# Two pairs of outputs of the last projection's second input half as seven block products, with residual rows at the end and moves around the pooled rows

## The reference, cut to what matters

```python
for l in range(DEPTH_2):
    u = rms_norm_2(h, norm_in_g[l])
    proj = jnp.einsum('bsd,de->bse', u, w_in[l])
    pool_x, pool_z, m_x, m_z = jnp.split(proj, ...)
    y_pool = pool_mixer(pool_x, pool_w[l], pool_scale[l]) * jax.nn.silu(pool_z)
    y_m = mlstm_branch(m_x, ...) * jax.nn.silu(m_z)
    y = jnp.concatenate([y_pool, y_m], axis=-1)
    h = h + jnp.einsum('bse,ed->bsd', y, w_out[l])
return rms_norm_2(h, norm_out_g)
```

## Time and profile before

| | before |
|---|---|
| time, median of 3 runs | 1710.2 us (1709.71 to 1710.64) |
| profiled execution | 1709.35 us, of which the profiler's span is 1707.6 |
| PE busy | 1664.8 us, 97% of the span, 8119 matmuls |
| DVE busy | 1277.2 us, 75% |
| ACT, POOL busy | 726.9 us (43%), 540.7 us (32%) |
| granted clock of PE, mean | 0.996 of full speed |

### The profile page before, as it was taken

One profiled execution on the slowest core, in us unless ns is written; L12 is line 12 of the kernel. 1 busy time (PEld: TensorE's weight loads), 2 busy tenths in 40 slices (PEclk: granted clock), 3 DMA queues, 4 the chain that ended last, 5 costly groups with the idle time before them and its releaser, 6 DMA issues.

```text
span 1707.6 us, 21819 instructions
## 1 busy us (share of the span) xinstructions
PE 1664.8 (97%) x8119; PEld 1375.5 (81%) x8119; DVE 1277.2 (75%) x1556; ACT 726.9 (43%) x933; POOL 540.7 (32%) x409
## 2 busy tenths in 40 slices
PE   8999999999999999999999999999999999999997
PEld 6888888887788888887788877788788788878885
DVE  7987888435677777777775799878888367789764
ACT  7211113225556655566622423511124667683203
POOL 5344544332201011111022323335344322217541
PEclk9999999999999999999999999999999999999998
DMA  6012125141010111101432354112226611344432
GB/s 231 25 75 75 46 91 209 62 169 42 25 38 1 37 38 38 36 3 38 166 113 99 113 183 149 64 68 81 75 88 202 244 50 63 124 162 159 173 111 99
DMA packets 51321, 164.93 MB, mean 97 GB/s; under 512 B 6272, under 2 KB 6912, under 8 KB 50960
## 3 DMA queue, kind: packets, MB, share of 16 engines
q1 hardware_dynamic: 50928, 163.01, 26.8%
q10 hardware_dynamic: 288, 0.52, 0.1%
HBM read 122.49 MB, written 41.03 MB: 96 GB/s over the span
## 4 chain that ended last, share of the span: by engine, by line
PE 81%; DVE 13%; ACT 3%; issue 2%; DMA 0%; POOL 0%; SPq 0%; DVEq 0%; POOLq 0%; ACTq 0%
PE pair L1212 27%; PE pair L1737 10%; PE pair L1399 9%; PE pair L1473 9%; PE pair L1536 5%; PE aux L1509 4%; PE pair L1522 3%; PE pair L1903 1%; PE aux L1688 1%; DVE stat_b L2995 1%; PE pair L1223 1%; PE pair L1888 1%; PE pair L1231 1%; PE aux L1649 1%; PE aux L1859 1%
## 5 line engine op out<-in xcount | busy, mean ns | idle before, releaser
L1046 POOL CAST w_hi<-w_raw 128x1024 fp32r<-128x1024 f32 x66 | 81.0, 1228 | 751.5 <-issue 561.7
L1048 POOL TENSOR_TENSOR w_lo<-w_raw,w_hi 128x1024 fp32r<-128x1024 f32 x66 | 173.1, 2622 | 5.3
L1212 PE MATMUL pair<-op_hi,w_hi 128*128 128x512 f32 x446 | 138.7, 392 | 1.0 <-ACTq L185 1.0
L1212 PE MATMUL pair<-op_lo,w_hi 128*128 128x512 f32 x446 | 137.9, 391 | 0.0
L1212 PE MATMUL pair<-op_hi,w_lo 128*128 128x512 f32 x446 | 137.7, 390 | 0.0
L2210 ACT ACTIVATE pt_hi<-pair 128x1024 fp32r<-128x1024 f32 x60 | 61.6, 1027 | 126.6 <-issue 84.3
L2627 DVE TENSOR_TENSOR pt_lo<-pair,pt_hi 128x1024 fp32r<-128x1024 f32 x60 | 73.5, 1225 | 52.0 <-ACT pt_hi L2210 48.5
L1473 PE MATMUL pair<-opb_hi,w_hi 128*128 128x512 f32 x256 | 101.9, 398 | 1.1 <-DVEq L185 0.6
L1212 PEld LDWEIGHTS pair<-op_hi,w_hi 128*128 128x128 f32 x446 | 83.8, 189 | 21.6 <-issue 3.0
L1473 PE MATMUL pair<-opb_hi,w_lo 128*128 128x512 f32 x256 | 100.2, 391 | 0.0
L1473 PE MATMUL pair<-opb_lo,w_hi 128*128 128x512 f32 x256 | 99.8, 390 | 0.0
(11 more groups left out here) (544 smaller groups left out, 4417.3 us busy)
## 6 DMA issues: line engine op xcount, KB each, us to landing
w_raw<-weight_units SPq DMA_DIRECT2D x106, 512.0 KB, 4.5
xa<-x_t SPq DMA_DIRECT2D x15, 512.0 KB, 7.4
x_dram<-xa SPq DMA_DIRECT2D x8, 512.0 KB, 6.3
xc<-x_dram SPq DMA_DIRECT2D x8, 512.0 KB, 7.8
x_dram<-xc SPq DMA_DIRECT2D x8, 512.0 KB, 2.8
u_dram<-u_rows SPq DMA_DIRECT2D x8, 512.0 KB, 5.8
c_dram<-c_rows SPq DMA_DIRECT2D x8, 512.0 KB, 2.8
t_raw<-x_dram SPq DMA_DIRECT2D x4, 1024.0 KB, 5.7
```

The lines of the kernel that those rows point to most:

```text
L1046: pool.tensor_copy(w_hi[:, half, :], w_raw[:, u % RAW, :]).then_inc(w_hi_done, 1)
L1048: pool.tensor_tensor(w_lo[:, half, :], w_raw[:, u % RAW, :], w_hi[:, half, :], ALU.subtract).then_inc(w_split, 1)
L1212: mm = pe.matmul(acc[:, cols], w, x[:, kx, cols], start=(first and k == 0 and n == 0), stop=(last and k == KT - 1 and n == 2))
```

## The change

1. `PAIRED3` gains offsets 10 and 12: outputs 2, 3 and 4, 5 of the second input half are made as pairs. Units 8 and 9 stay whole, 14 and 15 stay halves. For this SP loads four blocks of 1 MB from `y3_dram` (`load_block4`), DVE makes four block sums and their lo parts (`block4_sum`, `block4_low`), ACT the hi parts, and `pair4_add` adds each block product straight onto `xf`; P6, P7, P3 and P4 of PE wait for such an addition.
2. The residual rows are moved: 0 ahead of the splits of the second half, 1 into the first new pair, 2 to 4 into the second, 5 to 7 behind it.
3. The last additions of rows 6 and 7 stand ahead of `final(0, 4)` to `final(0, 7)` instead of ahead of the last two.
4. Beside the pooled rows of g = 3, `pair_low` of P3 and the sums around it move earlier on DVE, `mix(3, 1)` moves on PE from behind P3 to behind P1 of `FIRST_MZ`, and ACT's copy for `FIRST_MZ` moves ahead of `pool_silu`.

```diff
@@ -81,16 +81,18 @@
-PAIRED3 = (4, 6)
+PAIRED3 = (4, 6, 10, 12)
...
@@ -969,6 +983,15 @@
+            def load_block4(name):
+                rows, half = T_PARTS[T_SLOT[name]]
+                for n in (2 * KT - 2, 2 * KT - 1):
+                    sp.wait_ge(y_stored[n % 2], stored("y3", n))
+                sp.dma_start(t4_raw[name][:, :, :],
+                             y3_dram[KT + QUAD * rows:KT + QUAD * (rows + 1), :, half * HALF:(half + 1) * HALF]
+                             .rearrange("k p c -> p k c")).then_inc(t_loaded[rows], 16)
...
@@ -997,13 +1020,22 @@
             sp.wait_ge(product_done, product_at(PAIR3 + 1, "P1"))
             for k in range(KT, KT + 4):
                 load_low(k)
+            load_x_row(1)
             sp.wait_ge(product_done, product_at(PAIR3 + 1, "P6"))
             for k in range(KT + 4, 2 * KT):
                 load_low(k)
             weights_to(BASE[5] + 12)
-            for k in range(1, KT):
+            sp.wait_ge(product_done, product_at(PAIR3 + 1, "P7"))
+            load_block4("P5")
+            sp.wait_ge(unit_done, plain(SECOND[PAIR3 + 1] + 1))
+            load_block4("P7")
+            load_block4("P6")
+            sp.wait_ge(unit_done, plain(SECOND[PAIR3 + 1] + 2))
+            load_block4("P4")
+            weights_to(BASE[5] + 14)
+            for k in range(2, KT):
                 load_x_row(k)
-                weights_to(BASE[5] + 12 + k)
...
@@ -1720,6 +1754,8 @@
                     pe.wait_ge(pair_free[b], s // 2)
                 elif name in ("P5", "P2"):
                     pe.wait_ge(pair_free[1 - b], s // 2)
+                elif p >= PAIR4:
+                    pe.wait_ge(c22_added, added4_at(p, {"P6": "P1", "P7": "P6", "P3": "P5", "P4": "P7"}[name]))
                 elif name == "P6":
...
@@ -1775,7 +1811,7 @@
-                    if (p, name) in ((0, "P7"), (WIDE + 2, "P3")):
+                    if (p, name) in ((0, "P7"), (FIRST_MZ, "P1")):
...
                 pool_hi(2 * g + 1)
+                if g == 3:
+                    act.wait_ge(mix_done, 12)
+                    copy2_p1(FIRST_MZ, "mz")
                 pool_silu(2 * g, row_pairs["z"][0])
                 if g == 1:
                     copy2_p1(WIDE, "x")
-                if g == 3:
-                    act.wait_ge(mix_done, 12)
-                    copy2_p1(FIRST_MZ, "mz")
                 pool_silu(2 * g + 1, row_pairs["z"][1])
                 if g == 1:
                     copy2_p5(WIDE, "x")
...
@@ -3293,11 +3344,15 @@
+                        if g == 3 and i == 1 and span == 4:
+                            pair_low(p, "P3")
...
+                    if g == 3 and i == 1:
+                        pair_c22(p, row_pairs["z"])
...
-                    if beside:
+                    if beside and g != 3:
                         pair_low(p, "P3")
+                    if g == 3 and i == 1:
+                        pair_c11(p, row_pairs["z"])
+                        pair_first_add(p, row_pairs["z"])
+                        pair_sum(FIRST_MZ, 0)
+                        pair_sum(FIRST_MZ, 1)
...
@@ -3335,16 +3395,22 @@
+                if g == 3:
+                    pair_low(after, "P5")
+                    pair_sum(after, 2)
+                    pair_low(after, "P6")
+                    pair_first_scale(rows, scaled_a)
                     pair_second_row(p, rows, scaled_a)
                     pair_sum(after, 3)
                 pool_output(2 * g, rows[0])
...
@@ -3590,6 +3656,35 @@
+            def block4_sum(name):
+                minuend, other = {"P5": ("P7", "P5"), "P7": ("P6", "P7"), "P6": ("P6", "P5"), "P4": ("P4", "P6")}[name]
+                for rows in range(2):
+                    if rows == 0 or name != "P5":
+                        dve.wait_ge(t_loaded[rows], T3_LOADED + 32)
+                link(dve.tensor_tensor(t4_raw[name][:, :, :], t4_raw[minuend][:, :, :], t4_raw[other][:, :, :],
+                                       ALU.subtract), t_summed)
+            def block4_low(name):
+                dve.wait_ge(t_hi_made, T_HI0 + 2 * T3 + ("P5", "P7", "P6", "P4").index(name) + 1)
+                link(dve.tensor_tensor(t4_lo[name][:, :, :], t4_raw[name][:, :, :], t4_hi[name][:, :, :],
+                                       ALU.subtract), t_low)
+            def pair4_add(p, name):
+                e, b = SECOND[p] - BASE[5] - KT, bank(SECOND[p])
+                cols = slice(0, HALF) if name in ("P1", "P2", "P4") else slice(HALF, S)
+                dst = xf[:, e + (name in ("P5", "P7", "P4")), cols]
+                done = c22_added if name in ADDED4 else None
+                if name in ("P3", "P4"):
+                    dve.wait_ge(unit_done, plain(SECOND[p] + (1 if name == "P3" else 2)))
+                else:
+                    dve.wait_ge(product_done, product_at(p, name))
+                link(dve.tensor_tensor(dst, accumulator2(p, name), dst, ALU.add), done)
+                if name in ("P3", "P4"):
+                    signal(pair_free[1 - b if name == "P3" else b])
...
@@ -3681,14 +3763,73 @@
-            RESIDUAL_AT = ((1, 2), (3, 4), (5, 6), (7,), (), ())
+            pair_low(PAIR3 + 1, "P7")
+            dve.wait_ge(r_loaded, 16)
             residual(0)
-            for k in range(KT - 2):
-                if k >= 1:
-                    accumulate(3, k - 1, sq_f, acc_f)
-                whole_sum(k)
-                for n in RESIDUAL_AT[k]:
-                    residual(n)
+            pair_low(PAIR3 + 1, "P3")
+            y_low(8)
+            y_low(9)
+            pair_c11(PAIR3 + 1, partial_rows(PAIR3 + 1))
+            y_low(10)
+            y_low(11)
+            pair_c22(PAIR3 + 1, partial_rows(PAIR3 + 1))
+            y_low(12)
+            pair3_first_row(PAIR3 + 1)
+            y_low(13)
+            y_low(14)
+            pair3_second_row(PAIR3 + 1)
+            y_low(15)
+            for name in ("P5", "P7", "P6"):
+                block4_sum(name)
+            for n in range(3):
+                pair_sum(PAIR4, n)
+            whole_sum(0, x_done)
+            block4_sum("P4")
+            block4_low("P5")
+            pair_low(PAIR4, "P5")
+            block4_low("P6")
+            whole_sum(1, None)
+            pair_low(PAIR4, "P6")
+            pair_sum(PAIR4, 3)
+            pair4_add(PAIR4, "P1")
+            block4_low("P7")
+            pair4_add(PAIR4, "P5")
+            pair_low(PAIR4, "P7")
+            pair4_add(PAIR4, "P6")
+            pair_low(PAIR4, "P3")
+            block4_low("P4")
+            pair4_add(PAIR4, "P2")
+            for n in range(2):
+                pair_sum(PAIR4 + 1, n)
+            pair4_add(PAIR4, "P7")
+            pair_sum(PAIR4 + 1, 2)
+            pair4_add(PAIR4, "P3")
+            residual(1, x_done)
+            pair_low(PAIR4 + 1, "P5")
+            pair4_add(PAIR4, "P4")
+            pair_low(PAIR4 + 1, "P6")
+            pair4_add(PAIR4 + 1, "P1")
+            pair_sum(PAIR4 + 1, 3)
+            accumulate(3, 0, sq_f, acc_f)
+            pair4_add(PAIR4 + 1, "P5")
+            pair_low(PAIR4 + 1, "P7")
+            pair4_add(PAIR4 + 1, "P6")
+            pair_low(PAIR4 + 1, "P3")
+            residual(2, x_done)
+            pair4_add(PAIR4 + 1, "P2")
+            accumulate(3, 1, sq_f, acc_f)
+            pair4_add(PAIR4 + 1, "P7")
+            residual(3, x_done)
+            pair4_add(PAIR4 + 1, "P3")
+            residual(4, x_done)
+            pair4_add(PAIR4 + 1, "P4")
+            accumulate(3, 2, sq_f, acc_f)
+            residual(5, x_done)
+            accumulate(3, 3, sq_f, acc_f)
+            residual(6)
+            accumulate(3, 4, sq_f, acc_f)
+            residual(7)
             accumulate(3, KT - 3, sq_f, acc_f)
             half_sum(KT - 2, 0)
             half_accumulate(0)
...
@@ -3704,11 +3845,11 @@
-            for k in range(2, KT - 2):
+            for k in range(2, KT - 4):
                 final(0, k)
             half_accumulate(1)
             half_sum(KT - 1, 1)
-            for k in range(KT - 2, KT):
+            for k in range(KT - 4, KT):
                 final(0, k)
```

More of the change, by code:

```diff
@@ L2588, in _ @@
                 y3_hi(k)
+            for n, name in enumerate(("P5", "P7", "P6", "P4")):
+                block4_hi(n, name)
             for k in range(KT - 2):
@@ L3639, in _, with residual @@
             pair_sum(PAIR3 + 1, 3)
[L3640 to L3655 removed]
+            def residual(k, done=None):
                 dve.wait_ge(x_loaded[k], 64)
```

59 lines of the change are left out of this document (35 added, 24 removed).

## The result

The changed kernel takes 1737.28 us (median of 4, 1733.86 to 1737.52) against 1710.42 of before: a ratio of 1.0152, 95% interval 1.0139 to 1.0165. It is slower, as forecast, but by 26.9 us instead of 17.3, and 4.3 us above the end of the range. The profiled execution took 1737.32 us, with a span of 1735.5.

A forecast was written before the change was run, and what follows sets the result against it. The prediction took PE, with 81% of the chain, as the bound. To the profiled 1709.35 us it added +20.0 for the tail and -2.1 for the pooled rows, 1727.2; it said 1727.5, range 1716 to 1733.

The forecast's parts named there:

- The sign: Whole kernel: the change makes it slower; slower by more than 0.2% had a chance of 0.91.
- the two big mechanisms: Last projection: PE waits 6.7 us at P5 of the first new pair and 12.7 us at the first statistics.
- P5's wait: First new pair: P5 waits 6.7 us for `whole_sum(1)`, behind the block landing and DVE's list.
- the estimate from the page: Block loads: 4.4 us for 1 MB by the skill's formula, giving a P5 wait of 4.5 and 1725.0 us in all.
- The row train: Residual rows through one buffer: steps of 5.87 us make the first statistics wait 12.7 us.
- the first rival: Residual rows: the row buffer doesn't bind, the statistics wait 3.6 us, the whole is 1716.5; chance 0.07.
- Pooled rows: Pooled rows: the 3.20 us wait and low clock go, a new wait of some 2.7 comes: -2.1 us.
- The bound that I gave: Pooled rows: the gain lies between -0.4 us, if the clock falls anyway, and -5.0, if no new wait comes.
- Small waits in the two pairs: New pairs and units 14 and 15: short PE waits for DVE additions and weights, together 3.5 us.
- The end: From the statistics to the end: +0.8 us, with 1.7 of low clock and -0.85 from the finals' order.

The follow-up runs named there:

- The buffers: The changed kernel with five more buffers for residual rows, so rows 3 to 7 load without waiting for the single buffer: 1729.22 us, ratio 1.0109.
- a better one: The changed kernel with `whole_sum(1)` ahead of block P6's lo part and the sum of P4 behind P5's lo part: 1732.13 us, ratio 1.0125.
- the mended two pairs: The changed kernel with the second row first beside the pooled rows, five more residual row buffers and `whole_sum(1)` ahead of block P6's lo part: 1722.26 us.
- one move: The kernel before with only `pair_low` of P3 moved ahead of the last doubling step beside the pooled rows: 1710.12 us, ratio 0.9997.
- with its companions: The kernel before with only the moves beside the pooled rows of g = 3 (part 4 of the change): 1711.77 us, ratio 1.0005.
- the same with one more line swapped: The kernel before with the pooled-row moves, and the `pair_second_row` operation that empties P5's accumulator put first: 1706.92 us, ratio 0.9976.
- the last one: The two pairs with all mends, without the DVE work of residual rows 4 to 7 (output lacks those residuals): 1712.42 us, ratio 1.0010.
- the first kernel with one pair: The changed kernel without pooled-row moves, with one new pair (offset 12) and residual rows between whole units: 1724.72 us, ratio 1.0076.
- the second: The one-pair kernel with unit 11's sum moved up, some residuals and lo parts moved, and the mended pooled rows: 1715.20 us, ratio 1.0022.

## Why the prediction was wrong

The sign and the two big mechanisms were right, and their sizes nearly so. **P5's wait** (6.7 forecast) was 7.53: counted from unit 8, the sum of P7 began after 12.2 us, forecast 11.8, and from there to P5 it took 20.1, forecast 19.4 with dispatch, since DVE's operations there ran 2.7 us longer than undisturbed and not the 2.1 that I played. That the landing fits so well is partly luck: from the first load of `o_raw` to the last landing the queue took 29.7 us, forecast 27.1, but it began 1.0 earlier than I had it, and unit 8, from which the wait counts, came 1.5 late itself. The landing went as the rows said, not by the estimate from the page that I had set beside them: the four blocks took these times from issue to landing:

```profile
DMA to landing us min/median/max: 10.1/11.5/12.9
```

From the formula of the Trainium skill ("DMA: Bandwidth & Descriptors", section "Anatomy of one DMA — SWDGE (gpsimd) path") comes an estimate of 4.4 us for one transfer of 1 MB; the trace doesn't agree where the queue is full. **The row train** (12.7, of which the terms as written give 12.6) was 12.2, with loads of 3.30 to 3.38 us on the chain and steps of 5.97 to 6.11 from one of residuals 4 to 7 to the next (5.87 forecast). DVE's idleness ahead of these rows, forecast as some 3.3 us each, was only 1.35 to 2.63, since additions and running sums ran while the load was under way. The buffers took off 5.6 us of the wait, though, not all: behind the train stood DVE's own list, which I had put at a wait of 3.6 us in the first rival and which measured 6.6. That rival, that the buffer doesn't bind, is refuted by the same run.

The missing 10.0 us of span come from these steps:

- **"Pooled rows ... I take 0.4 + 1.73 = -2.1."** This is the step that failed in kind, 3.7 us. The wait of "some 2.7 us" was 3.14, and "it stays under the length after which the clock fell" was wrong: the clock fell again, and P5 and P6 took 8.36 us for 24 matmuls. The bound that I gave, -0.4 "if the clock falls anyway", wasn't a bound either: P1 and `mix(3, 1)` started some 0.2 us late each, and a spell of some 7 us at low clock, where before had one of some 3.4, cost 2.7 us and not the 1.73 of before. That made it +1.6.
- **"Small waits in the two pairs ... 3.5."** The waits were 0.61, 0.45, 0.43, 1.77 and 0.29, together 3.55. But each start after a wait cost some 0.28 us more: the overlap of the first matmul with the one ahead (0.17), and a longer first product (3.00 us for 12 matmuls against 2.88). The prediction has no term for it. With six such starts that is 1.7 us; the longer wait of P5 and 0.2 more of low clock make the 2.7 of the table.
- **The operations that I moved without a price.** The change puts lo parts of `o_raw` ahead of the last additions of the pair at offset 6, beside POOL's splits of units 8 and 9. The prediction puts this at nothing, without a reason. DVE's timeline after, at that pair's last additions:

```profile
1601.88 3.20 DVE L2670 TENSOR_TENSOR o_lo<-o_raw,o_hi 128x1024 fp32r<-128x1024 f32 x2
1605.11 0.69 DVE L3185 TENSOR_TENSOR xf<-pair,xf 128x512 f32<-128x512 f32 x1
```

  The two lo parts took 3.20 us where two undisturbed ones take 2.5; P4 waited 0.70 us for the addition behind them, and unit 8 0.34, with their restarts 1.5 us in all.
- **2.0 us that have nothing to do with the change's places:** +1.4 at 817 us (last section) and +0.6 spread over 330 us.
- The end was 0.4 over, for the low clock after the statistics' wait lasted longer; the row train gave 0.3 back.

The range failed because it was built from variants of the two big terms and took the small ones, and the stretches without a price, as exact. All of them err to one side.

**What the pairs are up against**, which my sum held in pieces but not as a whole: DVE. These are the windows from unit 8 to the statistics, before (from 2 us ahead of unit 8) and with the mended two pairs; behind the span stand busy us of PE, PEld, DVE, ACT and POOL:

```profile
1602.00:1683.00 81.00, 81.00 (x359) 67.16 (x358) 52.79 (x37) 9.66 (x11) 30.87 (x15) 1.00 0.23 80
```

```profile
1602.00:1694.00 92.00, 77.66 (x325) 61.87 (x326) 83.91 (x67) 14.67 (x11) 41.45 (x26) 0.96 0.27 99
```

DVE was busy 65% of the time before (52.79 of 81 us) and 91% with the pairs (83.91 of 92). The 31 us that came to it are more than the 28 that it had idle, and its 84 us don't fit into the 76 that would be left if PE saved its 5.4 and never waited. The order decides where PE waits, and a better one gave back 3.6 us at P5; but the volume stays, and no version with a new pair came under the kernel before. That no order or placing could do so is argued from these sums, not shown.

## What to carry to other kernels

Before matrix products are saved at the price of sums on another engine, add up that engine's whole stretch, with what a neighbour holds it up, not only the operations ahead of the first wait: at 65% busy there was no room for 31 us more in 81, of which the block sums and their lo parts, which come to mind first, are some 18.6 (an estimate, eight at 2.33). When one late operation is moved up, ask for the next user of everything that it passes, and for what the old stall hid: here one move gave nothing that the medians show, with its companions neither, and the same with one more line swapped gave 3.9 us. What frees a buffer goes ahead of what prepares the next one.

## What the runs showed of the hardware that I had not expected

The same wait was followed by a lower clock in one execution and not in the other. At 806 us both kernels run the same instructions, and PE waits 2.50 us in the one and 2.51 in the other. Before:

```profile
804.00:808.00 4.00, 1.96 (x16) 1.96 (x17) 3.83 (x6) 2.83 (x4) 0.00 (x0) 1.00 0.00 0
808.00:812.00 4.00, 4.00 (x28) 3.60 (x28) 3.57 (x5) 2.89 (x3) 0.00 (x0) 1.00 0.00 0
```

After:

```profile
804.00:808.00 4.00, 1.92 (x9) 1.92 (x10) 3.83 (x6) 2.87 (x4) 0.00 (x0) 0.73 0.00 0
808.00:812.00 4.00, 4.00 (x28) 3.89 (x28) 2.87 (x4) 1.49 (x2) 0.00 (x0) 0.84 0.00 0
```

The matmul that follows the next short wait starts at 817.08 before and at 818.52 after, 1.44 us later. Over the 14 profiled executions of all kernels, with waits of 2.50 to 2.52 us there, the granted clock fell in 9. So it is no property of the change, and single executions of kernels of this length differ by such steps: the medians are safer than a difference of two traces.

After waits of 2.5 to 3.0 us the clock fell sometimes: not after the 2.98 us in the kernel with one move nor the 3.01 us of the last one, but after 2.86 us at P4 in the first kernel with one pair and after 2.67 us at P7 in the second, where a window shows 0.58:

```profile
1660.00:1664.00 4.00, 3.35 (x8) 2.70 (x9) 3.90 (x4) 0.43 (x1) 1.57 (x2) 0.58 0.01 2
```

After the waits from 3.10 us on (3.10 to 3.21, 3.46, 3.8, 6.6 and longer) it fell each time, but for the 7 us with which every execution starts, and after 1.8 and less never. I had taken one instance as a threshold. Where I worked out the time lost, it was 1.4 to 2.7 us a time. A wait that is shortened to 2.7 us may thus have saved its length alone.
